# Which engine divides the attention weights by their row sums: VectorE or GpSimd

## The chip, the cores and the metric

The kernel runs on one core of a Trainium2 chip. Its time is the device time of one execution in microseconds (us). TensorE (PE in the profile, with its weight loads as PEld), VectorE (DVE), ScalarE (ACT), GpSimd (POOL) and SyncE (SP, which issues most DMAs) each run their own list of instructions in order and meet through semaphores.

## The reference, cut to what matters

The program computes two transformer-like blocks over 512 tokens of width 1024. The first block has an attention branch with 8 heads of width 128 over 2 key/value heads, in which each query keeps 128 selected causal keys, and a state-space branch. The second block follows with banded attention, a delta rule and a retrieval of experts. Only this line of the first block's attention matters here:

```python
sc = jnp.einsum("btgrd,btjgd->btgrj", qb, ks).astype(jnp.float32) * scale
sc = jnp.where(valid[:, :, None, None, :], sc, -jnp.inf)
pr = jax.nn.softmax(sc, axis=-1).astype(vs.dtype)
return jnp.einsum("btgrj,btjgd->btgrd", pr, vs)
```

The softmax is computed as exp(score - row maximum), summed by row, and multiplied by the reciprocal of the sum. That multiplication is what the change moves.

## The kernel before, in words

`build` runs the stages one behind the other. In `attention_branch` they are the projections, the rotary embedding, the selection of keys, `attention_stage` (8 heads), and `attention_out_stage`, a projection whose weights come through a ring of buffers that SyncE fills ahead. Each stage is a block, and at its end the engines meet.

In `attention_stage` the 512 queries of a head are four tiles of 128 rows (i = 0 to 3). Tile i sees (i+1)*128 keys, so the operations on the tile `scores` have widths of 128, 256, 384 and 512. Two heads have room in `scores`, `probsT`, `row_top` and `row_sum`. The order is written out by hand on each engine:

- TensorE, for head h: the 10 transposes of the normalized weights of head h (L889), each tile i behind the count `normed`; the score products of head h+2 (L875); the products with the values of head h (L898), behind the copies of the transposed weights.
- VectorE, for head h: `softmax_out(h)` (the reciprocal of the row sums, L916, and the four multiplications, L919), the gate of head h-1 (L924), then `softmax_in(h+2)` (for each tile the scaled and masked scores, L910, and the negated row maximum, L912). `softmax_in(h+2)` waits for the score products of head h+2 and for the count `flipped`, which is raised when head h's transposes are done, because it overwrites head h's scores.
- ScalarE, for head h: the copies of the transposed weights to SBUF (L957), then the exponentials of head h+2 with their row sums (L945).
- GpSimd has nothing in this stage.

All heads but the last two therefore have one loop that runs through VectorE and TensorE: reciprocal and multiplications of head h, transposes of head h, score products of head h+2, `softmax_in(h+2)`, and again the reciprocal, of head h+1.

Of the kernel before, what the change touches and what calls it, by code (L numbers as in the profile page):

```python
# [10 lines left out]
ALU = mybir.AluOpType  # L11
# [3 lines left out]
P = 128  # L15
# [3 lines left out]
NT = T // P  # L19
# [11 lines left out]
AH, AKV, IH = 8, 2, 4  # L31
# [72 lines left out]
def post(eng, ins, sig):  # L104

    ins.then_inc(sig.sem, 1)
    sig.n += 1
    eng.wait_ge(sig.sem, sig.n)
# [731 lines left out]
def attention_stage(k, t):  # L840

    nc = k.nc
    scale = float(P) ** -0.5
    with ExitStack() as ctx:
        def sb(name, shape):
            return ctx.enter_context(nc.sbuf_tensor(name, shape, F32))


        s_at, p_at = [0, P, 3 * P, 6 * P], [0, 4 * P, 7 * P, 9 * P]
        s = sb("scores", [P, 2, 10 * P])  # L850
        pT = sb("probsT", [P, 2, 10 * P])
        top = sb("row_top", [P, 2, NT])
        den = sb("row_sum", [P, 2, NT])
        scored = ctx.enter_context(nc.semaphore("scores_made"))
        read = Signal(ctx, nc, "scores_read")
        topped = Signal(ctx, nc, "row_tops")
        exped = Signal(ctx, nc, "exps_made")
        normed = Signal(ctx, nc, "probs_normed")
        flipped = ctx.enter_context(nc.semaphore("probs_flipped"))
        copied = Signal(ctx, nc, "probsT_copied")  # L860
        valued = ctx.enter_context(nc.semaphore("values_mixed"))
        gated = Signal(ctx, nc, "outputs_gated")
        block = ctx.enter_context(nc.Block())

        place = [(4, 0), (5, 0), (6, 0), (6, 256)]

        @block.tensor
        def _(pe):
            def scores(h):
                for i in range(NT):  # L870
                    if h > 0:

                        pe.wait_ge(read.sem, NT * (h - 1) + i + 1)
                    w = (i + 1) * P
                    pe.matmul(k.bank[i][:, 0:w], t.qT[:, h, i * P:w], t.kT[:, h // 4, 0:w],  # L875
                              start=True, stop=True).then_inc(scored, 1)

            scores(0)
            scores(1)
            for h in range(AH):  # L880
                for i in range(NT):
                    pe.wait_ge(normed.sem, NT * h + i + 1)
                    if h > 0 and i == 0:

                        pe.wait_ge(copied.sem, NT * h)
                    for j in range(i + 1):
                        b, c = place[j]
                        c += (i - j) * P
                        last = pe.transpose(k.bank[b][:, c:c + P], s[:, h % 2, s_at[i] + j * P:s_at[i] + (j + 1) * P], k.const("ident"))  # L889
                last.then_inc(flipped, 1)  # L890
                if h + 2 < AH:
                    scores(h + 2)
                if h > 0:
                    pe.wait_ge(gated.sem, h)
                for j in range(NT):
                    pe.wait_ge(copied.sem, NT * h + j + 1)
                    v = t.kv[:, j, 256 + (h // 4) * P:256 + (h // 4 + 1) * P]
                    last = pe.matmul(k.bank[7][:, j * P:T], v, pT[:, h % 2, p_at[j]:p_at[j] + T - j * P], start=(j == 0), stop=(j == NT - 1))  # L898
                last.then_inc(valued, 1)

        @block.vector
        def _(dve):
            def softmax_in(h):
                for i in range(NT):
                    w = (i + 1) * P
                    dve.wait_ge(scored, NT * h + i + 1)
                    if h >= 2:

                        dve.wait_ge(flipped, h - 1)
                    post(dve, dve.scalar_tensor_tensor(s[:, h % 2, s_at[i]:s_at[i] + w], k.bank[i][:, 0:w], scale,  # L910
                                                       t.madd[:, i, 0:w], ALU.mult, ALU.add), read)
                    post(dve, dve.tensor_reduce(top[:, h % 2, i:i + 1], s[:, h % 2, s_at[i]:s_at[i] + w], AX, ALU.max, negate=True), topped)  # L912

            def softmax_out(h):
                dve.wait_ge(exped.sem, NT * (h + 1))
                post(dve, dve.reciprocal(den[:, h % 2, :], den[:, h % 2, :]), k.vstep)  # L916
                for i in range(NT):
                    w = (i + 1) * P
                    post(dve, dve.tensor_scalar(s[:, h % 2, s_at[i]:s_at[i] + w], s[:, h % 2, s_at[i]:s_at[i] + w], den[:, h % 2, i:i + 1],  # L919
                                                None, ALU.mult), normed)  # L920

            def gate(h):
                dve.wait_ge(valued, h + 1)
                post(dve, dve.tensor_tensor(t.oT[:, h, :], k.bank[7][:], t.zT[:, h, :], ALU.mult), gated)  # L924

            softmax_in(0)
            softmax_in(1)
            for h in range(AH):
                softmax_out(h)
                if h > 0:  # L930
                    gate(h - 1)
                if h + 2 < AH:
                    softmax_in(h + 2)
            gate(AH - 1)

        @block.scalar
        def _(act):
            def exps(h):
                for i in range(NT):
                    w = (i + 1) * P  # L940
                    act.wait_ge(topped.sem, NT * h + i + 1)
                    if h >= 2 and i == 0:

                        act.wait_ge(normed.sem, NT * (h - 1))
                    post(act, act.activation(s[:, h % 2, s_at[i]:s_at[i] + w], s[:, h % 2, s_at[i]:s_at[i] + w], ACT.Exp,  # L945
                                             bias=top[:, h % 2, i:i + 1], accum_out=den[:, h % 2, i:i + 1]), exped)

            exps(0)
            exps(1)
            for h in range(AH):  # L950
                act.wait_ge(flipped, h + 1)
                if h >= 2:

                    act.wait_ge(valued, h - 1)
                for j in range(NT):
                    b, c = place[j]
                    post(act, act.activation(pT[:, h % 2, p_at[j]:p_at[j] + T - j * P], k.bank[b][:, c:c + T - j * P], ACT.Copy), copied)  # L957
                if h + 2 < AH:
                    exps(h + 2)
# [30 lines left out]
def attention_branch(k):  # L990
    with ExitStack() as ctx:
        def sb(name, shape):
            return ctx.enter_context(k.nc.sbuf_tensor(name, shape, F32))

        t = Part()
        t.merged = k.merged
        t.zT = sb("silu_zT", [P, 8, T])
        t.kv = sb("k_v_rows", [P, NT, 512])
        t.ix = sb("index_rows", [P, NT, IDX_COLS])
        t.kT, t.qiT, t.kiT = sb("kT", [P, AKV, T]), sb("index_qT", [P, 2, T]), sb("index_kT", [P, T])  # L1000
        t.qT = sb("qT", [P, AH, T])
        with k.nc.sbuf_tensor("q_rows", [P, NT, D], F32) as t.q:
            attention_projection_stage(k, t)
            attention_rotary_stage(k, t)
        t.madd = sb("selected_add", [P, NT, T])
        selection_stage(k, t)
        t.oT = t.zT
        attention_stage(k, t)
        attention_out_stage(k, t)
# [2869 lines left out]
```

## Time and profile before

| | |
|---|---|
| median of 3 runs | 2863.87 us (2857.37 to 2867.46) |
| the profiled execution | 2856.65 us, its span 2854.5 us |
| attention stage with the last product before it | from 311 to 375 us of the span |
| TensorE busy over the span | 2099.5 us (74%) |
| VectorE busy over the span | 1711.7 us (60%) |
| ScalarE busy over the span | 920.8 us (32%) |
| GpSimd busy over the span | 850.0 us (30%), none of it in the attention stage |
| mean granted TensorE clock | 0.832 of full speed |

The span runs from the first to the last instruction of the core. A row of a timeline gives the start in us from the span's start, the length, the engine, the line, the operation, what it writes and reads, and in brackets the idle time ahead of it with what ended it; consecutive instructions of one line are merged into one row with their count. What the attention stage costs is read from its own stretch and not from the shares over the span, since the stages have different limits.

### The profile page before, as it was taken

What the parts mean: (1) busy time and instruction counts of PE and PEld (TensorE: products, weight loads), DVE (VectorE), ACT (ScalarE), POOL (GpSimd) and SP (SyncE); (2) the same over time, 40 slices, a digit from 0 to 9 for tenths busy, and PEclk for the clock granted to TensorE, in tenths of its full rate; (3) what the DMA queues carried; (4) which work ended last, traced back from release to release, by engine and by line L of the source; (5) the groups of instructions that cost most, each with busy time, mean ns of one, the idle gap of its engine ahead of it and who ended that gap; (6) DMA issues with size and microseconds to landing.
All of it is one profiled execution on the core that took longest, in us unless ns stands there. A gap on an engine that the chain in (4) does not pass through costs nothing. (4 is left out here: it accounts for less than half of the span.)

```text
span 2854.5 us, 28792 instructions
## 1 busy us (share of the span) xinstructions
PE 2099.5 (74%) x9374; PEld 1200.9 (42%) x9374; DVE 1711.7 (60%) x3785; ACT 920.8 (32%) x2546; POOL 850.0 (30%) x767
## 2 busy tenths in 40 slices
PE   7999899999998999978987757768654533333333
PEld 3444444445586668867653435436211300000000
DVE  2058824347734322544677887885577777787874
ACT  2012412236611232032545643444533322222220
POOL 0000000013300000000556665677654444444442
PEclk8999999999999999989997768879767755665565
DMA  7114102223454432123899887999999999999997
GB/s 321 62 75 177 59 32 109 88 81 97 144 221 186 169 148 91 57 89 135 289 374 385 295 321 254 350 410 411 383 421 421 419 421 420 420 414 410 416 412 318
DMA packets 154821, 735.36 MB, mean 258 GB/s; under 512 B 17280, under 2 KB 49424, under 8 KB 103472
## 3 DMA queue, kind: packets, MB, share of 16 engines
q0 software_dynamic: 103680, 536.92, 47.5%
q1 hardware_dynamic: 50704, 195.72, 18.4%
q8 instruction: 75, 1.23, 0.2%
q10 hardware_dynamic: 288, 0.89, 0.1%
q14 instruction: 74, 0.61, 0.1%
HBM read 726.05 MB, written 7.42 MB: 257 GB/s over the span
## 5 line engine op out<-in xcount | busy, mean ns | idle before, releaser
L3639 PE MATMUL bank<-ring,xT 128*32 128x512 f32 x1376 | 384.2, 902 | 326.1 <-DVE xT L3475 265.5
L3639 PE MATMUL bank<-second_arena,xT 128*32 128x512 f32 x672 | 262.4, 990 | 215.0 <-DVE xT L3475 201.6
L3452 DVE CUSTOM_DVE_ANT_0 ring<-ring,second_arena 128x1024 f32<-128x1024 f32 x280 | 343.6, 1227 | 109.5 <-DMA ring<-in_peer_experts,experts_stacked 73.7
L496 PE MATMUL bank<-hT,ring 128*128 128x512 f32 (+1 forms) x1040 | 368.6, 516 | 2.9 <-PEq L3777 1.8
L3452 DVE CUSTOM_DVE_ANT_0 second_arena<-second_arena 128x1024 f32<-128x1024 f32 x232 | 284.8, 1228 | 98.4 <-DMA second_arena<-in_peer_experts,experts_stacked 71.2
L3639 PEld LDWEIGHTS bank<-ring,xT 128*32 128x32 f32 x1376 | 69.2, 142 | 500.8 <-issue 500.0
L496 PEld LDWEIGHTS bank<-hT,ring 128*128 128x128 f32 x1040 | 196.4, 190 | 179.6 <-issue 169.8
L3367 POOL DMA_INDIRECT ring<-in_peer_experts,experts_stacked x164 | 180.1, 1098 | 236.3 <-PE bank L3639 186.5
L3367 POOL DMA_INDIRECT second_arena<-in_peer_expert_down,experts x92 | 101.6, 1104 | 480.1 <-DVE experts L3426 417.5
L3367 POOL DMA_INDIRECT ring<-in_peer_expert_up,experts_stacked x180 | 199.6, 1109 | 88.3 <-issue 50.0
L494 PE MATMUL bank<-ring,hT 128*128 128x512 f32 (+1 forms) x512 | 216.8, 583 | 10.8 <-DMA ring<-in_weights 9.9
L1511 POOL TENSOR_TENSOR xs_dt_decay<-xs_dt,end_decays 128x512 f32<-128x512 f32 x12 | 21.1, 1755 | 640.5 <-DVE xs_dt L1438 617.6
L3367 POOL DMA_INDIRECT second_arena<-in_peer_experts,experts_stacked x140 | 151.1, 1079 | 199.9 <-PE bank L3639 167.6
L3639 PEld LDWEIGHTS bank<-second_arena,xT 128*32 128x32 f32 x672 | 44.7, 152 | 319.0 <-issue 318.8
L3615 ACT ACTIVATE expert_dots<-expert_dots 128x4 f32<-128x4 f32 x76 | 15.6, 205 | 455.0 <-DVE expert_dots L3452 454.7
L3367 POOL DMA_INDIRECT ring<-in_peer_expert_down,experts x116 | 125.9, 1085 | 102.4 <-DVE expert_dots L3452 30.2
L494 PEld LDWEIGHTS bank<-ring,hT 128*128 128x128 f32 x512 | 98.0, 193 | 127.1 <-issue 113.8
L3574 ACT ACTIVATE xT<-expert_coefs 32x2 f32<-32x2 f32 x416 | 84.4, 203 | 108.9 <-DVE expert_coefs L3490 71.8
L1126 DVE SCALAR_TENSOR_TENSOR xbcT<-bank,cols,xbcT 128x511 f32<-128x511 f32 (+2 forms) x72 | 54.0, 749 | 102.4 <-ACT xbcT L1088 100.7
L3550 ACT ACTIVATE experts_stacked<-experts 32x4 int32<-32x4 int32 x512 | 105.8, 207 | 6.6
L1249 PE MATMUL bank<-hT,ring 128*128 128x512 f32 x240 | 105.6, 593 | 0.8 <-ACT silu_z_columns L1350 0.8
L2007 PE MATMUL bank<-second_arena,ring 128*128 128x256 f32 x384 | 94.0, 397 | 2.5 <-issue 2.5
(533 smaller groups left out, 3676.9 us busy)
## 6 DMA issues: line engine op xcount, KB each, us to landing
ring<-in_weights SPq DMA_DIRECT2D x66, 2048.0 KB, 8.2
ring<-in_weights SPq DMA_DIRECT2D x14, 1024.0 KB
second_arena<-in_weights SPq DMA_DIRECT2D x12, 1024.0 KB
decay<-acum_scratch SPq DMA_DIRECT2D x16, 512.0 KB, 5.7
decay<-acum_scratch SPq DMA_DIRECT2D x24, 128.0 KB, 3.4
ring<-in_peer_expert_up,experts_stacked POOLq DMA_INDIRECT x180
ring<-in_peer_experts,experts_stacked POOLq DMA_INDIRECT x164
second_arena<-in_peer_experts,experts_stacked POOLq DMA_INDIRECT x140
```

The costliest lines, as they stand in the source:

```text
L494: last = pe.matmul(held[i][:, 0:n], fixed[:, which * ring.depth + kk, i * P:(i + 1) * P], w[:, kk, 0:n], **flags)
L496: last = pe.matmul(held[i][0:wide, 0:self.width], w[:, kk, i * P:i * P + wide], fixed[:, which * ring.depth + kk, :], **flags)
L1126: ins = dve.scalar_tensor_tensor(t.xbcT[:, j, back:T], bank[:, 0:T - back], k.col("conv_w", (3 - back) * 24 + j), t.xbcT[:, j, back:T], AL ...
L1249: last = pe.matmul(k.bank[7][:], w[:, kk, j * P:(j + 1) * P], k.hT[:, kk, :], start=(kk == 0), stop=(kk == KD - 1))
L1511: post(pool, pool.tensor_tensor(xdec[:, i], xdt[:, i], bc(ends[:, i, 0, :], 2, tall), ALU.mult), side)
L2007: last = pe.matmul(k.bank[6 + b][:, (i % 2) * H2:(i % 2 + 1) * H2], w[:, kk, i * P:(i + 1) * P], fixed[:, which * KD + kk, :], start=(whic ...
L3367: pool.indirect_dma_start(out=space(n), out_offset=None, in_=table, in_offset=bass.IndirectOffsetOnAxis(ap=rows, axis=0),).then_inc(here[l ...
L3452: post(dve, dve.tensor_tensor_reduce(row, row, tokens, 1.0, 0.0, ALU.mult, ALU.add, dots[:, u % 2, at:at + 1]), dotted)
L3550: ins = act.activation(mine, experts[blocks(q), i, h * RK + 4 * x:h * RK + 4 * x + 4], ACT.Copy)
L3574: ins = act.activation(mine, coef[blocks(q), u % 2, 4 * x + 2 * n:4 * x + 2 * n + 2], ACT.Copy)
L3615: post(act, act.activation(mine, mine, ACT.Gelu), gelued)
L3639: last = pe.matmul(sums[i][half][blocks(q), :], diag[(u * RK + 4 * g + q) % DR], rows[q][:, half * 512:(half + 1) * 512], start=(h == 0 an ...
```

## The change

The reciprocals stay on VectorE, in a function of their own, `invert(h)`, and raise a new count, `inverted`. The four multiplications of each head go to a new GpSimd program, which waits for `inverted` and raises `normed`. The order on VectorE is now `invert(h)`, `gate(h-1)`, `softmax_in(h+2)`. All shapes, values, buffers, and the programs of TensorE, ScalarE and SyncE are the same.

```diff
+        inverted = Signal(ctx, nc, "row_sums_inverted")
         normed = Signal(ctx, nc, "probs_normed")
...
-            def softmax_out(h):
+            def invert(h):
                 dve.wait_ge(exped.sem, NT * (h + 1))
-                post(dve, dve.reciprocal(den[:, h % 2, :], den[:, h % 2, :]), k.vstep)
-                for i in range(NT):
-                    w = (i + 1) * P
-                    post(dve, dve.tensor_scalar(s[:, h % 2, s_at[i]:s_at[i] + w], s[:, h % 2, s_at[i]:s_at[i] + w], den[:, h % 2, i:i + 1],
-                                                None, ALU.mult), normed)
+                post(dve, dve.reciprocal(den[:, h % 2, :], den[:, h % 2, :]), inverted)
...
             for h in range(AH):
-                softmax_out(h)
+                invert(h)
                 if h > 0:
                     gate(h - 1)
                 if h + 2 < AH:
                     softmax_in(h + 2)
             gate(AH - 1)
+
+        @block.gpsimd
+        def _(pool):
+            for h in range(AH):
+                pool.wait_ge(inverted.sem, h + 1)
+                for i in range(NT):
+                    w = (i + 1) * P
+                    mine = s[:, h % 2, s_at[i]:s_at[i] + w]
+                    post(pool, pool.tensor_scalar(mine, mine, den[:, h % 2, i:i + 1], None, ALU.mult), normed)
```

## Rows read from the trace of the kernel before

**Rows 1.** Busy time by engine (windows: length, busy and count, clock, DMA), attention stage.
```profile
311.00:371.00 60.00, 48.92 (x200) 30.45 (x200) 50.12 (x112) 34.58 (x94) 0.00 (x0) 0.97 0.03 11
```

**Rows 2.** Timeline of VectorE, one head in the middle of the stage.
```profile
335.59 0.18 DVE L916 RECIPROCAL row_sum<-row_sum 128x4 f32<-128x4 f32 x1
335.80 1.65 DVE L919 TENSOR_SCALAR scores<-scores,row_sum 128x128 f32<-128x128 f32 x4
337.49 0.69 DVE L924 TENSOR_TENSOR silu_zT<-bank,silu_zT 128x512 f32<-128x512 f32 x1
338.48 0.29 DVE L910 SCALAR_TENSOR_TENSOR scores<-bank,selected_add 128x128 f32<-128x128 f32 x1 [0.30 <-PE bank L875]
...
342.67 0.18 DVE L916 RECIPROCAL row_sum<-row_sum 128x4 f32<-128x4 f32 x1
```

**Rows 3.** Timeline of TensorE over the same head.
```profile
336.14 2.02 PE L889 MATMUL bank<-consts,scores 128*128 128x128 f32 x10 [0.74 <-DVE scores L919]
338.00 2.32 PE L875 MATMUL bank<-kT,qT 128*128 128x128 f32 x8
340.16 2.32 PE L898 MATMUL bank<-probsT,k_v_rows 128*128 128x512 f32 x8
```

**Rows 4.** Timeline of ScalarE over the same head.
```profile
335.65 0.72 ACT L945 ACTIVATE scores<-scores,row_top 128x512 f32<-128x512 f32 x1 [0.72 <-DVE row_top L912]
...
338.25 1.85 ACT L957 ACTIVATE probsT<-bank 128x512 f32<-128x512 f32 x4 [1.79 <-issue]
```

**Rows 5.** Timeline of VectorE, the stage's first head.
```profile
320.83 1.66 DVE L919 TENSOR_SCALAR scores<-scores,row_sum 128x128 f32<-128x128 f32 x4
...
324.29 0.29 DVE L910 SCALAR_TENSOR_TENSOR scores<-bank,selected_add 128x128 f32<-128x128 f32 x1 [1.81 <-PE bank L875]
```

**Rows 6.** Timeline of all engines, the last head and the next stage's start.
```profile
366.76 1.65 DVE L919 TENSOR_SCALAR scores<-scores,row_sum 128x128 f32<-128x128 f32 x4
...
367.33 2.39 PE L898 MATMUL bank<-probsT,k_v_rows 128*128 128x512 f32 x8 [0.83 <-ACT probsT L957]
...
369.45 1.12 PEld L889 LDWEIGHTS bank<-consts,scores 128*128 128x128 f32 x10
...
375.32 0.58 SPq L173 DMA_DIRECT2D ring<-in_weights  x1
...
375.38 4.96 PE L496 MATMUL bank<-silu_zT,ring 128*128 128x512 f32 x11 [1.34 <-PEq L844]
```

**Rows 7.** Windows: busy time and granted clock around the stage's first transposes.
```profile
316.00:321.00 5.00, 0.84 (x2) 0.01 (x1) 4.63 (x11) 2.94 (x9) 0.00 (x0) 1.00 0.00 2
321.00:326.00 5.00, 4.83 (x18) 3.79 (x19) 2.92 (x9) 2.49 (x7) 0.00 (x0) 0.66 0.00 0
```

**Rows 8.** The tile scores: the multiplications of all heads, ns min/median/max.
```profile
L919 DVE TENSOR_SCALAR scores<-scores,row_sum x32: 286/387/488, 320.8 to 367.9; 128x128 f32<-128x128 f32 x8, 128x256 f32<-128x256 f32 x8, 128x384 f32<-128x384 f32 x8, 128x512 f32<-128x512 f32 x8
```

**Rows 9.** Timeline of GpSimd in later stages.
```profile
634.35 1.04 POOL L1517 TENSOR_TENSOR state<-state,end_decays 128x512 f32<-128x512 f32 x1 [5.41 <-issue]
...
637.62 1.90 POOL L1511 TENSOR_TENSOR xs_dt_decay<-xs_dt,end_decays 128x512 f32<-128x512 f32 x1
...
657.38 2.25 POOL L1523 TENSOR_TENSOR xbcT<-xbcT,y_carried 128x512 f32<-128x512 f32 x1 [9.44 <-DVE xbcT L1457]
659.71 1.04 POOL L1511 TENSOR_TENSOR xs_dt_decay<-xs_dt,end_decays 128x512 f32<-128x512 f32 x1
...
918.96 2.69 POOL L396 TENSOR_TENSOR hT<-xT,norm_rstd 128x256 f32<-128x256 f32 x3 [126.35 <-DVE norm_rstd L387]
```

**Rows 10.** Timeline of VectorE beside those GpSimd rows.
```profile
634.41 0.69 DVE L1454 TENSOR_TENSOR y_carried<-bank,decay 128x512 f32<-128x512 f32 x1
...
636.88 1.74 DVE L1443 TENSOR_TENSOR decay<-decay,cb_causal 128x1024 f32<-128x1024 f32 x1
...
659.72 3.26 DVE L1473 TENSOR_TENSOR xbcT<-xbcT,silu_z_columns 128x512 f32<-128x512 f32 x2 [1.22 <-POOL xbcT L1523]
...
917.13 1.75 DVE L387 RECIPROCAL norm_rstd<-norm_rstd 128x256 f32<-128x256 f32 x1 [4.79 <-ACT norm_rstd L413]
918.92 3.35 DVE L390 TENSOR_TENSOR hT<-xT,norm_rstd 128x256 f32<-128x256 f32 x5
```

## Prediction

> **What bounds the kernel now.** I read the windows of the attention stage first, because the shares over the whole span mix stages with different limits. From 311 to 371 us TensorE is busy 48.92 of 60 us and VectorE 50.12, GpSimd not at all, and DMA moves next to nothing [rows 1]. Two engines near 80% each can mean two engines that take turns, so the next view is VectorE's timeline over one head [rows 2]. The reader should see there that it repeats every 342.67 - 335.59 = 7.08 us and has one gap: 0.30 us ahead of L910, ended by TensorE's score product. TensorE's timeline has its own gap, 0.74 us ahead of the transposes, ended by VectorE's multiplications [rows 3]. So each engine waits for the other once per head, and the loop is one chain:
>
> - reciprocal, start to the next start: 335.80 - 335.59 = 0.21 us;
> - four multiplications: 1.65 us, to 337.45;
> - from there to `softmax_in(h+2)`: 338.48 - 337.45 = 1.03 us. In it TensorE does the last tile's transposes and the first score product; VectorE's gate of 0.69 us lies inside it and is free;
> - `softmax_in(h+2)` until the next reciprocal: 342.67 - 338.48 = 4.19 us.
>
> The sum is 7.08 us, the whole period, so nothing else is in the loop [rows 2]. ScalarE's last exponential of a head ends at 336.4 and its row sum is wanted only a period later, behind the reciprocal at 342.67 [rows 2, 4]; its copies are beside the score products. This head stands for the ones from 328 to 364 us.
>
> **The change part by part.** *What leaves VectorE.* Four multiplications per head, 1.65 us with their gaps. They look like relief for an engine that is busy 50 of 60 us, but the next thing in its queue besides the free gate is `softmax_in(h+2)`, which needs head h's transposes and the score products queued behind them, and these need the same multiplications. VectorE cannot use the freed time; it waits in it. And `invert(h+1)`, whose inputs were ready long before, stays queued behind `softmax_in(h+2)`, so GpSimd cannot start on head h+1 any earlier. The chain keeps its links, one of them changes its engine, and two handoffs are added or changed.
>
> *The link on GpSimd.* No row of before shows this operation on GpSimd. The nearest by engine is its two-tensor multiplication of 128x512, 1.04 us beside a VectorE instruction that reads PSUM and one SBUF tensor [rows 9, 10]. The four widths sum to 1280 columns, 2.5 times 512, so in proportion to the columns this is 2.60 us; two GpSimd instructions in a row stand 659.71 - (657.38 + 2.25) = 0.08 us apart [rows 9], three gaps more, 2.84 us. The new operation reads one tensor and a column instead of two tensors. On VectorE that makes 0.488 us at the widest against 0.69 for its two-tensor gate, a factor of 0.71 [rows 2, 8]; applied to 2.84 it gives 2.0 us. I take the middle, **2.4 us**, because the row on GpSimd itself is nearer by engine and the factor is nearer by operation. Bounds: below, VectorE's own 1.65 us is the nearest row of the same operation, and nothing in the trace excludes that GpSimd is as fast or somewhat faster on one tensor; with half the reads of the two-tensor rows it would need half their 2.84, 1.4 us. Above, the three instructions of 128x256 took 2.69 us, 0.90 each [rows 9], hardly less than the 1.04 of one twice as wide. Read as a fixed price per instruction this is 0.76 us + 0.14 per 256 columns, so 0.83, 0.90, 0.97 and 1.04, with three gaps 3.98 us. But VectorE ran two-SBUF-tensor instructions beside those three [rows 10], and where it did so in another place, at 636.88, GpSimd's 128x512 stretched from 1.04 to 1.90 us [rows 9, 10]. I take those 0.90 as mostly contention: 0.5 by proportion and the rest waiting.
>
> *Contention here.* Beside the moved instructions VectorE runs only the gate, which reads PSUM and one SBUF tensor like L1454, beside which GpSimd showed its 1.04 us [rows 9, 10]. So I charge nothing. If that is wrong it costs up to the gate's 0.69 us per head.
>
> *The Trainium skill on this price.* GPSIMD Engine Reference, section "4.1 Engine selection", says elementwise work belongs on VectorE, being about 2 times slower on GpSimd with two inputs, but roughly at line rate with one; its clock is stated as 1.2 GHz, so 1280 columns at one per cycle would be an estimated 1.1 us and the whole link about 1.3. Section "3.1 Elementwise — side-by-side cycle accounting" of the same page gives 1.8 cycles per element as the best of a tight loop, an estimated 1.9 us. No row here has a one-input operation on GpSimd. The two-input half of the rule is borne out: 1.04 us against 0.69.
>
> *Handoffs.* VectorE to GpSimd: L387 ended at 918.88 and GpSimd began at 918.96, 0.08 us [rows 9, 10], where VectorE to itself takes 335.80 - 335.77 = 0.03. GpSimd to a waiter: 657.38 + 2.25 = 659.63 to 659.72, 0.09 us [rows 9, 10], where TensorE now follows VectorE's first multiplication (335.80 + 0.29) at 336.14, in 0.05 [rows 2, 3, 8]. Together +0.10 us per head.
>
> *Per head and in sum.* 2.4 - 1.65 + 0.10 = **+0.85 us**, a period of 7.93 us. The first head has the same chain: its multiplications end at 322.49 and `softmax_in` follows at 324.29 [rows 5]. Heads 0 to 6 carry the link. In head 7 it is covered: its multiplications now end at 368.41, and TensorE comes to its transposes only at 369.45, behind the values of head 6 [rows 6]. That cover holds with the changed kernel as well: from the end of head 6's multiplications, about 365.8, TensorE needs 3.7 us to reach head 7, and GpSimd needs 2.4 for head 7. If it were gone (a link over 3.7 us), the excess would be added once. So 7 x 0.85 = **+6.0 us**.
>
> *Costed at nothing.* The extra semaphore and GpSimd's arrival at the stage's end: it finishes before TensorE's last products. ScalarE's wait for `normed` ahead of the exponentials comes behind its wait for `flipped`, which is later. On GpSimd nothing else is queued in this stage [rows 1]. No DMA is moved; SyncE's next load goes out when `attention_out_stage` begins, at 375.32, with the first product at 375.38 [rows 6], so this stage hides no transfer and what it loses is passed on in full. The granted clock is 0.97 over the stage [rows 1]; it fell, to a mean of 0.66 in one stretch, only behind one in which TensorE was busy 0.84 of 5 us [rows 7]. The new gaps are far shorter: idle time per head grows by 0.85 us, in pieces between the transposes.
>
> *Against the times.* The profiled execution took 2856.65 us and its span is 2854.5; with 6.0 more, 2862.7. It lies 7.2 us under the median of the runs, 2863.87, which is at the middle of a spread of 10 us. Nothing in the argument depends on that, so I add to the median: **2869.9 us**, +0.21%.
>
> **The rivals.**
>
> - *Fixed price per GpSimd instruction.* The link is 3.98 us, +2.43 per head, 7 x 2.43 = +17.0, and some 0.3 for head 7: 2881 us, slower. For it speaks that 256 columns cost 0.90 us and 512 cost 1.04 [rows 9]; against it the contention beside the 256s. It turns to "slower" once the link exceeds 1.65 - 0.10 + 8.6/7 = 2.78 us.
> - *GpSimd at line rate.* The link is 1.4 to 1.65 us, so -0.15 to +0.10 per head, -1.1 to +0.7 in all: 2863 to 2865, no change. For it in the rows speaks only that one tensor is read instead of two. It is the case that section 4.1 of the Trainium skill's GPSIMD Engine Reference describes for one input.
> - *The clock falls.* If the longer gaps pull TensorE to its lower level, the stretch from the last multiplication to `softmax_in` becomes that of the first head, 324.29 - 322.49 = 1.80 us instead of 1.03 [rows 2, 5]: 0.77 more for six heads, 4.6, and with the 6.0 it is +10.6: 2874.5, slower. Against it: before the clock fell TensorE had been busy 0.84 of 5 us [rows 7], and with the change its idle time would be about 0.74 + 0.85 of 7.9 us [rows 3].
> - *A first use of the operation on GpSimd costs something once.* By rows I bound it with GpSimd's longest instruction above, 2.25 us against 1.04 undisturbed [rows 9]: 1.2 more, 2871, still no change that can be told. Section "2.1 Instruction dispatch" of the same reference in the Trainium skill states about 6 us for GpSimd code that must first be loaded, which would be an estimated 2876; no row here shows it.
> - *The loss is absorbed later.* Then 2864. The trace shows no place that waits for an absolute time.
> - *Faster.* This would need over 1.2 us less per head. All that lies between the last multiplication and `softmax_in` is 1.03, so I know no mechanism for it.
>
> **How the numbers follow.** A measurement of this kernel can tell about 0.3% from no change, 8.6 us. Forecast, link 2.0 to 2.78 us, +3 to +8.6: 0.45. Line rate: 0.13. Absorbed: 0.02. First use: 0.03. These are "same", 0.63. Fixed price (link over 2.78): 0.25; clock: 0.08. These are "slower", 0.33. Unforeseen gain: 0.04. The range takes in line rate at the low end (2863, less 3 for the spread of the runs, of which the median of three takes a part) and the fixed price at the high end (2881): 2860 to 2882.
>
> **What would show it.** In the trace of the changed kernel: GpSimd's row for the moved line, four instructions spanning 2.4 us (2.0 to 2.8 confirms the forecast, 1.4 to 1.7 line rate, near 4 the fixed price; whether the 128-wide one costs much less than the 512-wide one tells proportion from fixed price). VectorE's wait ahead of L910, ended by TensorE, grows from 0.30 by 1.65 + 0.85 = 2.5 to about 2.8 us. The reciprocals stand 7.93 us apart. The time from GpSimd's last multiplication to L910 stays 1.03 + 0.04. The clock stays 1.00 in 326 to 371 us. The first product of L496 begins at about 381.3 instead of 375.38, and everything behind it is shifted by the same amount. I am wrong if VectorE starts `softmax_in` before GpSimd is done, or if the stage is longer and the span isn't.

## The result, and the profile after

The changed kernel takes 2895.04 us in the median of 4 runs (2888.23 to 2909.17) against 2861.93 for the kernel before, a ratio of 1.0121 with a 95% interval of 1.0079 to 1.0164: slower by 1.2%, where +0.21% was forecast, 2869.9 us in a range of 2860 to 2882. Measured again beside the last experiment it was 1.0123 (1.0090 to 1.0156). Its profiled execution took 2893.36 us, with a span of 2891.2.

The attention stage carries nearly all of it. From the stage's first scores on VectorE to the first product of the next stage it took 375.38 - 312.22 = 63.2 us before [rows 6, and the line of L910 at 312.22 below] and 405.66 - 312.28 = 93.4 us after: 30.2 us more. I call this the length of the stage below and give it for each kernel. First two rows of before, both from the timeline of VectorE; the second, the start of the state-space branch, is used under experiments 8 and 9:

```profile
312.22 0.29 DVE L910 SCALAR_TENSOR_TENSOR scores<-bank,selected_add 128x128 f32<-128x128 f32 x1 [1.03 <-PE bank L875]
...
432.43 0.17 DVE L1101 MEMSET ones_row<- 32x128 f32 x1 [1.08 <-PEq L3777]
```

After, the first scores of the stage start at 312.28 us, and TensorE's timeline has the first product of the next stage:

```profile
405.66 4.53 PE L496 MATMUL bank<-silu_zT,ring 128*128 128x512 f32 x10 [1.33 <-PEq L844]
```

The groups of GpSimd's instructions in the stage, by shape, after (busy us, mean ns, idle before):

```profile
L940 POOL TENSOR_SCALAR scores<-scores,row_sum 128x512 f32<-128x512 f32 x8 | 12.5, 1562 | 0.7
L940 POOL TENSOR_SCALAR scores<-scores,row_sum 128x384 f32<-128x384 f32 x8 | 9.9, 1242 | 0.7
L940 POOL TENSOR_SCALAR scores<-scores,row_sum 128x256 f32<-128x256 f32 x8 | 7.4, 922 | 0.7
L940 POOL TENSOR_SCALAR scores<-scores,row_sum 128x128 f32<-128x128 f32 x8 | 4.8, 603 | 361.2 <-DVE row_sum L917 361.1
```

Each step of 128 columns adds 320 ns, 2.5 ns per column, on 0.28 us. That is neither of the two readings in the prediction: the 128x512 costs 1.56 us, one and a half times GpSimd's own two-tensor row [rows 9], and the link is 4.61 us where 2.4 was forecast and 3.98 was the upper end.

One head on VectorE and GpSimd after, from their timelines (the answer to [rows 2]):

```profile
343.59 0.18 DVE L917 RECIPROCAL row_sum<-row_sum 128x4 f32<-128x4 f32 x1
344.32 0.69 DVE L921 TENSOR_TENSOR silu_zT<-bank,silu_zT 128x512 f32<-128x512 f32 x1 [0.54 <-PE bank L899]
350.24 0.29 DVE L911 SCALAR_TENSOR_TENSOR scores<-bank,selected_add 128x128 f32<-128x128 f32 x1 [5.23 <-PE bank L876]
...
351.09 0.42 DVE L911 SCALAR_TENSOR_TENSOR scores<-bank,selected_add 128x256 f32<-128x256 f32 x1 [0.24 <-PE bank L876]
...
352.12 0.56 DVE L911 SCALAR_TENSOR_TENSOR scores<-bank,selected_add 128x384 f32<-128x384 f32 x1 [0.15 <-PE bank L876]
...
354.75 0.18 DVE L917 RECIPROCAL row_sum<-row_sum 128x4 f32<-128x4 f32 x1
```

```profile
343.94 4.61 POOL L940 TENSOR_SCALAR scores<-scores,row_sum 128x128 f32<-128x128 f32 x4 [6.44 <-DVE row_sum L917]
355.10 4.61 POOL L940 TENSOR_SCALAR scores<-scores,row_sum 128x128 f32<-128x128 f32 x4 [6.55 <-DVE row_sum L917]
```

The reader should see that the two engines strictly alternate: GpSimd idles 6.44 us until the reciprocal, VectorE 5.23 us until the score product that stands behind GpSimd's work. The reciprocals of the first seven heads stand between 320.67 and 388.89 us, 11.37 us apart in the mean, against 7.22 before (7.08 in each interval but the first).

TensorE over the same head (the answer to [rows 3]), and its granted clock by windows (length, busy and count of PE, PEld, DVE, ACT and POOL, clock, DMA; the answer to [rows 7]):

```profile
344.60 0.33 PE L890 MATMUL bank<-consts,scores 128*128 128x128 f32 x1 [0.39 <-POOL scores L940]
345.61 0.44 PE L890 MATMUL bank<-consts,scores 128*128 128x128 f32 x2 [0.69 <-POOL scores L940]
346.95 0.55 PE L890 MATMUL bank<-consts,scores 128*128 128x128 f32 x3 [0.90 <-POOL scores L940]
348.60 1.12 PE L890 MATMUL bank<-consts,scores 128*128 128x128 f32 x4 [1.10 <-POOL scores L940]
349.51 3.38 PE L876 MATMUL bank<-kT,qT 128*128 128x128 f32 x8
```

```profile
321.00:326.00 5.00, 2.45 (x8) 1.36 (x9) 0.00 (x0) 0.55 (x2) 4.28 (x4) 0.50 0.00 0
...
341.00:371.00 30.00, 21.32 (x68) 12.64 (x66) 12.87 (x26) 10.63 (x30) 12.35 (x12) 0.82 0.00 0
```

TensorE waits ahead of every tile, never longer than 1.1 us in this head, and still the clock is 0.82 over 30 us, so it was at the lower of its two levels, 1.2 instead of 2.4 GHz, for part of the time. The eight score products, 2.32 us before [rows 3], take 3.38 in this head and up to 4.47 in others, and VectorE gets them late. From the end of GpSimd's last multiplication (343.94 + 4.61 = 348.55) to `softmax_in` it is 1.69 us instead of 1.03, and from there to the next reciprocal 4.51 instead of 4.19, with the two waits of 0.24 and 0.15 us shown above.

### The profile page after: what moved, and what is told of

It is laid out like the page before. It is cut to its first block and busy times, and to the rows that moved or that the text cites. A ratio compares the mean times of both kernels' runs of the same rounds, so it can differ in the third digit from the quotient of the medians.

```text
span 2891.2 us, 28800 instructions
## 1 busy us (share of the span) xinstructions
PE 2112.9 (73%) x9374; PEld 1209.3 (42%) x9374; DVE 1700.5 (59%) x3753; ACT 920.5 (32%) x2546; POOL 893.3 (31%) x799
## 5 line engine op out<-in xcount | busy, mean ns | idle before, releaser
L3373 POOL DMA_INDIRECT ring<-in_peer_expert_up,experts_stacked x180 | 205.9, 1144 | 90.8 <-issue 50.8
L940 POOL TENSOR_SCALAR scores<-scores,row_sum 128x128 f32<-128x128 f32 (+3 forms) x32 | 34.6, 1082 | 363.5 <-DVE row_sum L917 361.1
```

The costliest lines, as they stand in the source:

```text
L940: post(pool, pool.tensor_scalar(mine, mine, den[:, h % 2, i:i + 1], None, ALU.mult), normed)
L3373: pool.indirect_dma_start(out=space(n), out_offset=None, in_=table, in_offset=bass.IndirectOffsetOnAxis(ap=rows, axis=0),).then_inc(here[l ...
```

## The experiments

**1. The price of the operation.** GpSimd multiplies two tensors instead:

```diff
-post(pool, pool.tensor_scalar(mine, mine, den[:, h % 2, i:i + 1], None, ALU.mult), normed)
+post(pool, pool.tensor_tensor(mine, mine, den[:, h % 2, i:i + 1].broadcast_to([P, w]), ALU.mult), normed)
```

> As the changed kernel, but the four multiplications on GpSimd are written as a product of two tensors, the second being the column of reciprocals repeated along the row. Theory (the price is that of the operation with one tensor and a column, 0.28 us + 2.5 ns per column): the 128x512 takes 1.04 us as GpSimd's other two-tensor rows do, four of them 2.8 us instead of 4.6. The reciprocals then stand 8.3 us apart if the TensorE clock holds and up to 9.5 if it still falls; the first product of the next stage begins 8.5 to 15 us later than before (at 384 to 390 us) and not 30. Rival (GpSimd is slow here because of what runs beside it or how the tile lies): the 128x512 stays at 1.56 us and the stage at +30.

Measured: the stage is 391.68 - 311.8 = 79.9 us, +16.7, and the whole takes 1.0057 times the kernel before (1.0037 to 1.0076). The ratios below are meant in the same way. By shape:

```profile
L940 POOL TENSOR_TENSOR scores<-scores,row_sum 128x512 f32<-128x512 f32 x8 | 8.3, 1042 | 0.6
L940 POOL TENSOR_TENSOR scores<-scores,row_sum 128x384 f32<-128x384 f32 x8 | 6.6, 828 | 0.6
L940 POOL TENSOR_TENSOR scores<-scores,row_sum 128x256 f32<-128x256 f32 x8 | 4.9, 614 | 0.6
L940 POOL TENSOR_TENSOR scores<-scores,row_sum 128x128 f32<-128x128 f32 x8 | 3.2, 401 | 358.4 <-DVE row_sum L917 358.3
```

The 1.04 us is there, on the same tile in the same place, so the dearness belongs to the operation and not to its surroundings. The four make 3.11 us, not 2.8, because there is a part of 0.19 us per instruction beside 1.67 ns per column. The reciprocals stand 9.5 to 9.8 us apart but for one interval of 8.65, where a held clock would give 7.08 + 3.11 - 1.65 + 0.15 = 8.7 (the 0.15 is for the handoffs, see below); the clock is 0.87 from 326 to 371 us. So the 8.3 was too low, and the stage ended above the expected 8.5 to 15. The 128x256 at 614 ns also bears on the 0.90 us each of [rows 9], which the prediction took as mostly contention (0.5 us of its own and the rest waiting): 0.61 is the operation's own here, so some 0.29 is left for contention, which no run isolates.

**2. The clock.** TensorE fills its waits:

```diff
 for i in range(NT):
+    for _f in range(20 if h == 0 and i == 0 else i + 2):
+        pe.transpose(k.bank[6][:, 384:512], k.const("ident"), k.const("ident"))
     pe.wait_ge(normed.sem, NT * h + i + 1)
```

> As the changed kernel, but TensorE fills its waits for GpSimd with transposes of the identity into columns of a bank that nobody reads: 20 ahead of the first head, then 2, 3, 4 and 5 ahead of the four tiles of each head. Theory (1.2 us of the 4.3 us per head come from the lower TensorE clock, which TensorE's waits bring about): the clock stays at 1.00 through the stage, the reciprocals stand 7.08 + 2.96 + 0.1 = 10.15 us apart instead of 11.37, and the next stage begins 21 to 23 us later than before instead of 30. Rival (the rest beyond GpSimd's own time is a slow handoff from GpSimd): 11.4 us apart as before the filling, or more, and +30.

Measured: a stage of 399.04 - 312.1 = 86.9 us, +23.7, and 1.0072 (1.0047 to 1.0098) in all. Timeline of VectorE, of GpSimd, and the window that answers to those above:

```profile
331.36 0.18 DVE L919 RECIPROCAL row_sum<-row_sum 128x4 f32<-128x4 f32 x1
...
337.36 0.29 DVE L913 SCALAR_TENSOR_TENSOR scores<-bank,selected_add 128x128 f32<-128x128 f32 x1 [5.10 <-PE bank L876]
...
341.54 0.18 DVE L919 RECIPROCAL row_sum<-row_sum 128x4 f32<-128x4 f32 x1
```

```profile
331.71 4.62 POOL L942 TENSOR_SCALAR scores<-scores,row_sum 128x128 f32<-128x128 f32 x4 [6.28 <-DVE row_sum L919]
```

```profile
326.00:371.00 45.00, 35.75 (x175) 24.07 (x174) 22.01 (x47) 20.62 (x57) 17.37 (x16) 0.98 0.00 0
```

With more work on TensorE, none of it useful, the stage is 6.5 us shorter than in the changed kernel. The clock is 0.98 and four of the six intervals between reciprocals are 10.18 us (the other two 10.84 and 10.89), as expected: the old period, GpSimd's 4.61 for VectorE's 1.65, and 0.15 for the handoffs. The stage is a little over the expected 21 to 23. The rival, a slow handoff from GpSimd, falls: from its last multiplication, ending at 331.71 + 4.62 = 336.33, to `softmax_in` is 1.03 us, exactly as before. The clock did not hold everywhere (0.80 in 321 to 326 us, 0.81 in 371 to 380), and the added transposes cost something themselves: the ten of head 7 span 2.56 us with them, 1.25 without. So 6.5 us is the least that the clock costs.

**3. The place of the link.** VectorE takes the reciprocals one head earlier:

```diff
+            invert(0)
             for h in range(AH):
-                invert(h)
+                if h + 1 < AH:
+                    invert(h + 1)
                 if h > 0:
                     gate(h - 1)
```

> As the changed kernel, but VectorE takes the reciprocals of head h+1 before the scores of head h+2, so GpSimd can multiply head h+1 while VectorE works on head h+2. Theory (the moved work costs time only because it stands in the loop of each head): GpSimd's 4.6 us per head leave the loop, TensorE with 6.3 us per head becomes the bound, the reciprocals stand 6.3 to 6.8 us apart and the next stage begins at 370 to 375 us, up to 5 us earlier than in the kernel before. Rival (GpSimd's rate bounds the stage wherever it stands, or the clock falls in any case): 8 us apart or more, and a later start than before.

Measured: GpSimd still spends 4.61 us per head, but the stage is 376.48 - 313.8 = 62.7 us, 0.5 shorter than before the change and 30.7 shorter than with it. Timeline of VectorE and GpSimd:

```profile
353.56 0.18 DVE L917 RECIPROCAL row_sum<-row_sum 128x4 f32<-128x4 f32 x1 [1.01 <-ACT scores L953]
...
359.65 0.18 DVE L917 RECIPROCAL row_sum<-row_sum 128x4 f32<-128x4 f32 x1 [1.01 <-ACT scores L953]
```

```profile
353.90 4.61 POOL L942 TENSOR_SCALAR scores<-scores,row_sum 128x128 f32<-128x128 f32 x4 [1.48 <-DVE row_sum L917]
```

The period is 6.09 us, under the expected 6.3 to 6.8, and the rival's 8 is out; the first period, whose head still waits for GpSimd, is 11.87. The next stage begins at 376.48, not at 370 to 375, mostly because the whole stage stands 1.6 us later in this trace. A new wait has come in, though, 1.01 us for ScalarE's last exponential, which had been hidden by a period. The whole kernel measured 1.0025 (1.0008 to 1.0042), 7 us over the kernel before with a stage no longer than that one's; 2.5 of them are the entry into the next branch (below), the rest I can't place.

**4. The same order without GpSimd.** The multiplications stay on VectorE and move with the reciprocals one head earlier:

```diff
+            softmax_out(0)
             for h in range(AH):
-                softmax_out(h)
+                if h + 1 < AH:
+                    softmax_out(h + 1)
```

> As the kernel before, with the multiplications on VectorE, but VectorE does reciprocal and multiplications of head h+1 before the scores of head h+2. Theory (in the kernel before the two engines take turns, 0.30 us and 0.74 us of waiting per head): both waits go but for what the busier engine leaves, the reciprocals stand 6.3 to 6.6 us apart instead of 7.08, and the next stage begins 3 to 5 us earlier than before, at 370 to 372 us. Rival (the two engines are each near their own bound and the gaps only move): 6.9 to 7.1 us apart and no change.

Measured: both theories missed. The stage is 382.44 - 313.75 = 68.7 us, 5.5 longer than before, and the total can't be told from no change, 1.0006 (0.9989 to 1.0024). Timeline of VectorE:

```profile
331.10 0.18 DVE L916 RECIPROCAL row_sum<-row_sum 128x4 f32<-128x4 f32 x1 [1.01 <-ACT scores L947]
331.32 1.65 DVE L919 TENSOR_SCALAR scores<-scores,row_sum 128x128 f32<-128x128 f32 x4
333.00 0.69 DVE L924 TENSOR_TENSOR silu_zT<-bank,silu_zT 128x512 f32<-128x512 f32 x1
...
338.89 0.18 DVE L916 RECIPROCAL row_sum<-row_sum 128x4 f32<-128x4 f32 x1 [1.01 <-ACT scores L947]
```

I had not asked what the moved reciprocals would wait for. Everything is now in VectorE's queue one behind the other, 0.22 for the reciprocal, 1.68, 0.73 for the gate, 4.15 for the scores and the 1.01 of waiting, 7.79 us. In this order the freed time on VectorE is worth something (6.09 us a head in experiment 3 against 7.79), which it was not in the changed kernel.

**5. A constant as the factor.** The division by the row sums is left out of what this kernel computes.

```diff
-post(pool, pool.tensor_scalar(mine, mine, den[:, h % 2, i:i + 1], None, ALU.mult), normed)
+post(pool, pool.tensor_scalar(mine, mine, 1.0, None, ALU.mult), normed)
```

> As the changed kernel, but GpSimd multiplies by the constant 1 instead of the column of reciprocals; the division by the row sums is left out of what is computed. Theory (the price of 0.28 us + 2.5 ns per column is GpSimd's loop for this operation, whatever the second factor): 602, 922, 1242 and 1562 ns again, within 5%. Rival (reading the factor from a column of the tile is what makes it dearer than the two-tensor form at 1042 ns): the 128x512 falls to 1.04 us or below and the four of them to 3.1 us or less.

```profile
L940 POOL TENSOR_SCALAR scores<-scores 128x512 f32<-128x512 f32 x8 | 11.9, 1488 | 0.7
L940 POOL TENSOR_SCALAR scores<-scores 128x384 f32<-128x384 f32 x8 | 9.3, 1168 | 0.7
L940 POOL TENSOR_SCALAR scores<-scores 128x256 f32<-128x256 f32 x8 | 6.8, 848 | 0.7
L940 POOL TENSOR_SCALAR scores<-scores 128x128 f32<-128x128 f32 x8 | 4.2, 528 | 363.1 <-DVE row_sum L917 363.0
```

The 320 ns per 128 columns stay; the column as a factor costs 74 ns per instruction. The expected 5% holds for the widest alone (4.7% lower); the others are 6, 8 and 12% lower. The slope is that of the operation. The stage is 404.37 - 314.1 = 90.2 us.

**6. The pieces put together.** Head 0 on VectorE, the rest on GpSimd in the two-tensor form, and the gate ahead of the early reciprocal, to cover its wait. Of the edit only the order is shown:

```diff
...
             for h in range(AH):
-                invert(h)
                 if h > 0:
                     gate(h - 1)
+                if h + 1 < AH:
+                    invert(h + 1)
                 if h + 2 < AH:
                     softmax_in(h + 2)
...
```

> The pieces put together: head 0 is divided on VectorE as in the kernel before, heads 1 to 7 on GpSimd in the two-tensor form, and VectorE does the gate of head h-1, then the reciprocals of head h+1, then the scores of head h+2. Theory (with GpSimd's link out of the loop and the reciprocal's wait for ScalarE covered by the gate, TensorE is the bound): reciprocals 5.9 to 6.3 us apart, the clock at 1.00 from 326 us on, the next stage 4 to 6 us earlier than in the kernel before, counted from the stage's first scores, of which the later entry into the state-space branch takes 2.5 back; the total 0 to 4 us under the kernel before, which this measurement can hardly tell from no change. Rival (something else than GpSimd's time and the clock holds the early order back): the next stage no earlier than in the kernel before.

Measured: 366.23 - 313.1 = 53.1 us, 10.1 shorter than before, and 2847.89 us against 2857.92 beside it, a ratio of 0.9972 (0.9953 to 0.9990): faster than both kernels, though the kernel before by only 0.3%. The stage gained 10.1 us where 4 to 6 were expected, and the 2.5 us at the entry into the state-space branch that were to be taken back were not lost (below). Timelines of VectorE and of TensorE:

```profile
346.61 0.18 DVE L917 RECIPROCAL row_sum<-row_sum 128x4 f32<-128x4 f32 x1 [0.28 <-ACT scores L958]
...
352.02 0.18 DVE L917 RECIPROCAL row_sum<-row_sum 128x4 f32<-128x4 f32 x1 [0.28 <-ACT scores L958]
```

```profile
350.69 1.25 PE L890 MATMUL bank<-consts,scores 128*128 128x128 f32 x10
351.79 2.32 PE L876 MATMUL bank<-kT,qT 128*128 128x128 f32 x8
353.95 2.32 PE L899 MATMUL bank<-probsT,k_v_rows 128*128 128x512 f32 x8
356.10 1.25 PE L890 MATMUL bank<-consts,scores 128*128 128x128 f32 x10
```

The period is 5.41 us, half a microsecond under what I expected, and TensorE has no gap left: it is the bound. I had taken TensorE's need from its busy time in the kernel before, where the ten transposes span 2.02 us [rows 3]; much of that was waiting between tiles. Without waits they span 1.25. No kernel has this order with all multiplications on VectorE, so that the gain is GpSimd's and not the order's is not shown by a run. An estimate from the terms of experiment 4 speaks for GpSimd: 0.22 + 1.68 + 0.73 + 4.15 and the 0.28 of waiting that is left make 7.06 us per head, no better than before.

**7. The same with the dear form of the operation.** The only edit to experiment 6 is the reverse of experiment 1.

> As e6_combined, but GpSimd multiplies in the form of the changed kernel (one tensor and a column, 4.61 us per head instead of 3.11). Theory (once off the loop of a head, GpSimd's time matters only if it exceeds what TensorE needs, 5.41 us per head): from the middle heads on the reciprocals stand 5.4 to 5.8 us apart, and the next stage begins 53 to 57 us behind the stage's first scores, against 53.1 in e6_combined, 63.2 in the kernel before and 93.4 in the changed one. Rival (the operation's price counts in any place): 1.5 us more per head than in e6_combined, 6.9 apart, and 63 us or more.

Measured: 371.02 - 314.2 = 56.8 us, within the expected 53 to 57, and 0.9975 (0.9958 to 0.9993). From the middle heads on its reciprocals stand by turns 5.42 and 5.74 us apart. Off the loop, 1.5 us more per head on GpSimd cost at most 3.7 us for seven heads; on the loop (the changed kernel against experiment 1) they cost 93.4 - 79.9 = 13.5.

**8 and 9. The entry into the state-space branch.** Behind the attention's output projection all engines meet, and there the changed kernel loses once more. Timeline of TensorE and VectorE after, and the window behind it:

```profile
463.45 14.93 PE L496 MATMUL bank<-hT,ring 128*32 128x512 f32 x30 [2.62 <-PEq L3783]
463.50 0.17 DVE L1107 MEMSET ones_row<- 32x128 f32 x1 [1.87 <-PEq L3783]
```

```profile
463.00:468.00 5.00, 4.55 (x7) 1.07 (x8) 0.17 (x1) 0.20 (x1) 0.00 (x0) 0.66 0.74 254
```

VectorE waited 1.08 us there before, now 1.87; TensorE's clock falls, and the first row of `minus_abs` comes 2.5 us later, counted from the output projection's first product (440.4 - 375.38 = 65.0 before, 473.2 - 405.66 = 67.5 after). Two kernels were to find the cause:

```diff
 exped = Signal(ctx, nc, "exps_made")
+spare = Signal(ctx, nc, "row_sums_inverted")
```

> The kernel before with one more semaphore taken in the attention stage and used by nobody. In every kernel with a GpSimd program in that stage the engines enter the state-space branch later: TensorE waits 2.62 us there instead of 1.83, the clock falls to 0.66 as a mean of the next 5 us, and 2.5 us are lost from the first product of the attention's output to the state-space branch. Theory (it is GpSimd's program, not the semaphore): 1.83 us, clock 1.00, 65.0 us from the first product of L496 to the first row of minus_abs. Rival (one more semaphore makes the clearing longer): 2.62 us and 67.5.

```diff
+        own = sb("own", [P, 4])
...
+        @block.gpsimd
+        def _(pool):
+            pool.memset(own[:], 1.0)
```

> The kernel before with a GpSimd program in the attention stage that does one memset of 128x4 and nothing else. Theory (that GpSimd has any program in the stage makes the entry into the state-space branch later): TensorE waits 2.62 us there, the clock falls to 0.66 in the next 5 us, 67.5 us from the first product of the attention's output to minus_abs. Rival (it needs GpSimd's work late in the stage, or the extra semaphore): 1.83 us, 1.00 and 65.0.

Both measured TensorE's wait at 1.83 us and 65.0 us to `minus_abs`, with no delay. Each was executed once, in 2861.20 and 2860.70 us. So it is neither an additional semaphore nor the mere presence of a GpSimd program. Experiments 6 and 7, which have both and a full program, wait 1.85 us too, while the changed kernel (twice) and experiments 1, 2, 3 and 5 wait 2.62. Among the kernels with a full GpSimd program only these two divide head 0 on VectorE, which leaves GpSimd 28 multiplications instead of 32, and take the gate ahead of the reciprocal. No run tests either, so the cause stays open. The stage of the kernel with the spare semaphore was 377.48 - 314.4 = 63.1 us, that with the memset 379.58 - 313.9 = 65.7, of which 1.7 are one group of value products at the lower clock: this much a stage can vary by the clock alone.

**10. The changed kernel again.**

> The changed kernel once more, for a second trace and more times. Theory (30 us in the attention stage, 2.5 at the entry into the state-space branch, the rest of the difference of the two profiled executions from where the clock happened to be low in the second block): 93 to 94 us from the stage's first scores to the next stage, 11 to 12 us between reciprocals, a median 28 to 36 us over the kernel before. Rival (part of the 30 us was chance): a stage below 90 us.

A stage of 407.60 - 314.1 = 93.5 us, the reciprocals 11.1 to 11.9 us apart, 67.5 us to `minus_abs`, and 1.0123 (1.0090 to 1.0156). The medians are 38.1 us apart, a little over the expected 28 to 36.

## Why the prediction was wrong, point by point

- *The loop.* Right. It said that VectorE cannot use the freed time, that GpSimd cannot start earlier because the reciprocal is queued behind `softmax_in`, and that the link's time is therefore paid per head. Experiment 3 moves only the reciprocals, GpSimd still takes its 4.61 us per head, and the whole 30 us go.
- *The link on GpSimd.* This term failed. It was put at 2.4 us with bounds of 1.4 and 3.98, and is 4.61. The step that failed is the transfer from another operation: the two-tensor row was scaled down by the factor that VectorE shows between its two forms. On GpSimd the factor goes the other way, 1.56 against 1.04 us at 128x512. Both bounds assumed that one tensor costs no more than two. With 4.61 in the prediction's own sum it is 7 x 3.06 = 21.4 us, and 0.9 more for head 7, which did not come (below).
- *The rule of a page.* What section "4.1 Engine selection" of the Trainium skill's GPSIMD Engine Reference states for one input, "roughly line-rate", does not hold here: by the clock that the page states in section "1. Specifications", 1.2 GHz, 2.5 ns per column is an estimated 3 cycles. For two inputs the section states about 2 times slower than VectorE; the rows show 1.5 (1.04 against 0.69 us), so the prediction's "borne out" is right in direction only. The section's advice to keep elementwise work on VectorE does hold for this chain, but not for the order of experiment 6.
- *The clock.* Given as a rival with a chance of 0.08 and 0.77 us per head, and taken as excluded by TensorE's short idle pieces. It came in: behind the first head the reciprocals stand (388.89 - 332.54) / 5 = 11.27 us apart, 1.1 beyond the link and the handoffs (10.18, experiment 2), and the stage loses at least 6.5 us by experiment 2. The prediction also treated this and the dear link as alternatives, though the second brings about the first: a longer link means a less busy TensorE.
- *Handoffs.* Put at +0.10. From the reciprocal's start GpSimd begins 0.35 us later where VectorE took 0.21, and TensorE follows GpSimd's first multiplication (332.89 + 0.60) at 333.55, 0.06. Together +0.15, 0.05 more than the prediction had.
- *Contention.* Right: nothing. The four multiplications take 4.61 us in the first head, which has no gate beside them, and in the later ones, which have.
- *First use of the operation.* Right: the first head's four take 4.61 us like all others.
- *Head 7 and its cover.* TensorE reaches head 7 at 399.85, GpSimd ended at 389.23 + 9.31 = 398.54. Covered, but only because TensorE itself was late.
- *Passed on in full, costed at nothing behind the stage.* Right for the output projection: its last product is used at 430.65 us before and at 460.94 after, still 30.3 apart. Wrong by 2.5 us at the entry into the next branch.
- *Against the times.* The two profiled executions differ by 36.7 us. 30.2 and 2.5 are accounted for. Some 8 us arise around 1250 us of the span (27.9 us of difference ahead of it, 35.8 behind), in the second block, where the same matmuls ran at the lower clock after and for the most part not before. Windows of before, then of after:

```profile
1235.00:1255.00 20.00, 18.88 (x142) 14.98 (x143) 10.67 (x19) 10.27 (x17) 0.00 (x0) 0.91 0.26 93
```

```profile
1263.40:1283.40 20.00, 19.46 (x86) 14.68 (x88) 6.02 (x10) 4.48 (x9) 0.00 (x0) 0.50 0.01 1
```

The other traces took 314 to 316 us from the first row of `band_top` to the first of `expert_dots`, as after did, and before 307, so before's profiled execution was a favourable one; between the entry and there the difference shrinks from 32.8 to 27.9 us. That stretch varied by 5 us over all traces (599 after, 604 before, the others 600 to 602), which I can't place. By medians the loss is 33 us, which the 32.7 explain within the interval.

In sum: 21.4 for the link by the prediction's own rule, at least 6.5 for the clock, some 2 of the stage that are not separated (an estimated 1.3 of them, 2.56 - 1.25, are what the added transposes of head 7 cost experiment 2, so the clock cost at least that much more), 2.5 at the entry, whose cause is open.

## What to carry to other kernels

When two engines take turns, moving work to a third does not relieve the chain; it only changes the price of one link. Look first for what can be issued earlier so that the link leaves the loop, and then name what the earlier instruction will wait for (experiment 4). The price of an operation on another engine is taken from that same operation or bounded generously on both sides, since the order of two forms on one engine says nothing of the other. And whatever makes TensorE wait more is also asked for what the clock will do.

## What the runs showed of the hardware

- GpSimd multiplies a float32 tensor of 128 rows by one factor per row in 0.28 us + 2.5 ns per column (603 to 1562 ns), by a constant 74 ns faster, and two tensors, the second being that column repeated along the row, in 0.19 us + 1.67 ns per column (401 to 1042 ns): the form with more to read is the faster one.
- TensorE's clock fell in a stage where it was busy 21.3 of 30 us and, in the head shown, no wait was longer than 1.1 us; useless transposes in the waits brought it from 0.82 to 0.98 and the stage down by 6.5 us.
